# Two mixers: the convolved keys and queries activated and squared at item 28 of the attention loop instead of after it, the filler products dropped, and the result stored in five parts

## The reference, cut to what matters

```
def gated_deltanet(pc, conv_w, a_log, dt_bias, o_norm):
    q, k, v, z, b_in, a_in = split_cols(pc, GDN_SPLITS)
    qkv = silu(causal_dwconv(concatenate([q, k, v]), conv_w))
    q, k, v = split(qkv, 3)
    q = l2_normalize(heads(q), 1e-6) * GDN_HEAD ** -0.5
    k = l2_normalize(heads(k), 1e-6)
    beta = sigmoid(b_in)
    g = -exp(a_log) * softplus(a_in + dt_bias)
    o = chunk_gated_delta_rule(q, k, heads(v), g, beta)
    return rms_norm(o, o_norm) * silu(heads(z))

def l2_normalize(x, eps):
    return x * rsqrt(sum(x * x, axis=-1) + eps)

for l in range(2):
    x = x + 0.5 * swiglu(rms_norm(x) ...)
    x = x + concatenate([attention, rwkv7, gated_deltanet]) @ w_out[l]
    x = x + 0.5 * swiglu(rms_norm(x) ...)
# then two layers of the second block, each of which updates x twice;
# the last one ends with   x = x + g2 * swiglu_2(...)   and x is the output
```

## Time and profile before

| | |
|---|---|
| median of 3 runs | 3575.18 us (3574.53 to 3580.99) |
| profiled execution | 3576.05 us |
| its span, first to last instruction | 3574.3 us |
| PE busy | 3423.1 us (96%) |
| DVE, ACT, POOL busy | 1408.8, 1249.7, 1660.1 us |
| mean granted PE clock | 0.978 of full |
| mixer stretches without tiles | from 575.75 (237.4 us) and from 1766.37 (241.5 us) |
| the store of the result | issued at 3566.68, lands 7.1 us later |

### The profile page before, as it was taken

The page is one execution under the profiler, slowest core; times in us unless marked ns, Lnnn a source line. Parts: engine busy times, 40 slices in busy tenths (PEclk is TensorE's granted clock), DMA queues, the critical chain, the costliest instruction groups (busy, mean ns, idle before and its releaser), DMA issues.

```text
span 3574.3 us, 47700 instructions
## 1 busy us (share of the span) xinstructions
PE 3423.1 (96%) x17140; PEld 2813.0 (79%) x17140; DVE 1408.8 (39%) x2740; ACT 1249.7 (35%) x1881; POOL 1660.1 (46%) x2052
## 2 busy tenths in 40 slices
PE   7999998799999999999878999999899999999999
PEld 6888775688888888887658888888767888888887
DVE  4431477855321322236787442215563110341100
ACT  3222335534222422233463432223533332433321
POOL 5765542004665566644300266644403555435553
PEclk9999998899999999999889999999999999999999
DMA  4443221003443344322100144432202322213222
GB/s 176 145 141 112 83 77 50 16 1 107 148 145 118 118 147 143 125 91 77 65 25 1 57 145 146 135 101 89 77 1 71 100 94 98 73 65 101 99 94 94
DMA packets 100319, 335.25 MB, mean 94 GB/s; under 512 B 10800, under 2 KB 16592, under 8 KB 100064
## 3 DMA queue, kind: packets, MB, share of 16 engines
q1 hardware_dynamic: 83920, 277.83, 23.4%
q10 hardware_dynamic: 16272, 55.65, 4.6%
HBM read 330.78 MB, written 2.65 MB: 93 GB/s over the span
## 4 chain that ended last, share of the span: by engine, by line
issue 40%; POOL 32%; PE 27%; DVE 1%; POOLq 0%; ACT 0%; DVEq 0%
POOL w_lo L654 32%; PE ps L2159 7%; PE ps L2160 7%; PE ps L2161 7%; PE ps L2937 1%; PE ps L2916 0%; PE ps L2182 0%; PE ps L2925 0%; PE ps L2183 0%; PE ps L2187 0%; PE ps L3027 0%; DVE stat L2064 0%; DVE sq L2057 0%; PE ps L3033 0%; PE ps L2917 0%
## 5 line engine op out<-in xcount | busy, mean ns | idle before, releaser
L654 POOL TENSOR_TENSOR w_lo<-w_raw,w_hi 128x256 fp32r<-128x256 f32 x2040 | 1653.4, 843 | 1890.9 <-ACT w_hi L697 1884.3
L2159 PE MATMUL ps<-h_hi,w_hi 128*128 128x512 f32 x2624 | 1030.8, 393 | 0.9 <-ACT mem L899 0.9
L2161 PE MATMUL ps<-h_hi,w_lo 128*128 128x512 f32 x2624 | 1021.6, 389 | 0.0
L2160 PE MATMUL ps<-h_lo,w_hi 128*128 128x512 f32 x2624 | 1021.1, 389 | 0.0
L697 ACT ACTIVATE w_hi<-w_raw 128x1024 fp32r<-128x1024 f32 x510 | 538.5, 1058 | 931.5 <-DMA w_raw<-in_tiles 931.5
L2159 PEld LDWEIGHTS ps<-h_hi,w_hi 128*128 128x128 f32 x2624 | 492.6, 188 | 118.2 <-issue 14.3
L2160 PEld LDWEIGHTS ps<-h_lo,w_hi 128*128 128x128 f32 x2624 | 492.7, 188 | 104.4 <-issue 3.4
L2161 PEld LDWEIGHTS ps<-h_hi,w_lo 128*128 128x128 f32 x2624 | 492.5, 188 | 102.3
L2160 PE MATMUL ps<-a_lo,w_hi 128*128 (+1 forms) x1120 | 435.7, 389 | 0.0
L2159 PE MATMUL ps<-a_hi,w_hi 128*128 (+1 forms) x1056 | 410.8, 389 | 0.0
L2161 PE MATMUL ps<-a_hi,w_lo 128*128 (+1 forms) x1056 | 410.8, 389 | 0.0
(11 more groups left out here) (473 smaller groups left out, 3646.2 us busy)
## 6 DMA issues: line engine op xcount, KB each, us to landing
w_raw<-in_tiles SPq DMA_DIRECT2D x510, 512.0 KB, 3.3
ada_raw<-in_ada_tiles ACTq DMA_DIRECT2D x96, 512.0 KB, 3.3
x<-in_x_t SPq DMA_DIRECT2D x2, 1024.0 KB, 6.4
sq<-in_cond ACTq DMA_DIRECT2D x4, 512.0 KB, 4.0
mem<-gates SPq DMA_DIRECT2D x8, 256.0 KB, 4.0
out_t<-x SPq DMA_DIRECT2D x1, 2048.0 KB, 7.1
consts<-in_consts SPq DMA_DIRECT2D x1, 1280.0 KB, 12.6
core_mem<-gates SPq DMA_DIRECT2D x8, 128.0 KB, 2.8
```

The source lines that it names most:

```text
L654: ins = nc.gpsimd.tensor_tensor(w_lo[:, s, part], w_raw[:, s, part], w_hi[:, s, part].bitcast(F32), ALU.subtract)
L2159: nc.tensor.matmul(bank, wh, hi, start=first, stop=False, skip_group_check=True)
L2160: nc.tensor.matmul(bank, wh, lo, start=False, stop=False, skip_group_check=True)
L2161: return nc.tensor.matmul(bank, wl, hi, start=False, stop=last, skip_group_check=True)
```

## The change

Four things are done, in both layers (the last one once):

- Keys after the convolution go to units 24 and 25 (`U_KG`), free once the convolution is done, and `k * delta` goes to units 9 and 10 (`U_KD`).
- ACT activates and squares keys and queries in `meanwhile(28)` instead of `meanwhile(31)`; the Sqrt table and both roots stay in `meanwhile(31)`.
- PE sums the squares in `meanwhile(29)`, into bank 1, and the 15 filler products are gone. The spread of the keys in `meanwhile(33)` waits for the first inverse ahead of chunk 0 and for the second ahead of chunk 1.
- The result is stored as one DMA of 1 MB (`x` 4 to 7, after the first four updates) and four of 256 KB, each after its own update.

```
-                    if i == 31:
+                    if i == 28:
                         act.wait_ge(S["conv_ready"], l + 1)
                         for at, unit in ((2, U_KG), (0, U_QG)):
                             link(nc.scalar.activation(mem[:, unit:unit + 2, :], core_mem[...], ACT.Silu))
                             nc.scalar.activation(mem[:, U_NORMED + at:...], mem[:, unit:unit + 2, :], ACT.Square).then_inc(S["head_sq"], 1)
+                    if i == 31:
                         load_sqrt()
-                        head_roots(2, 2, 1.0, EPS_NORM, 2)
+                        head_roots(1, 2, 1.0, EPS_NORM, 2)
+                        head_roots(1, 2, 1.0, EPS_NORM)
...
             def recurrences(l, updates):
-                head_roots(3, 2, 1.0, EPS_NORM)
...
+                    if i == 29:
+                        pe.wait_ge(S["g_taken"], l + 1)
+                        for at in (2, 0):
+                            pe.wait_ge(S["head_sq"], due("head_sq"))
+                            head_sums(mem_units(U_NORMED + at, U_NORMED + at + 1), 1, at).then_inc(S["head_sum"], 1)
                     if i == 33:
-                        pe.wait_ge(S["max_ready"], i0 + len(ITEMS))
-                        pe.wait_ge(S["g_taken"], l + 1)
-                        for _ in range(10):
-                            nc.tensor.matmul(ps[:, 1, 0:P], const("ident"), const("ones"), start=True, stop=True)
-                        for at, bank in ((2, 2), (0, 3)):
-                            pe.wait_ge(S["head_sq"], due("head_sq"))
-                            head_sums(...)
-                        for _ in range(5):
-                            nc.tensor.matmul(...)
-                        pe.wait_ge(S["head_inv"], due("head_inv"))
                         for c in range(2):
+                            pe.wait_ge(S["head_inv"], due("head_inv"))
                             head_spread(mem[:, U_NORMED + 2 + c, :], c).then_inc(S["head_spread"], 1)
...
+            sp.wait_ge(S["x_ready"], updated - KD // 2)
+            sp.dma_start(out_t[:, low:high, :], x[:, low:high, :]).then_inc(S["out_stored"], 16)
+            for d, k in enumerate(last_half):
+                sp.wait_ge(S["x_ready"], updated - KD // 2 + d + 1)
+                sp.dma_start(out_t[:, k, :], x[:, k, :]).then_inc(S["out_stored"], 16)
```

More of the change, by code:

```diff
@@ L219, in build_program @@
         soft = mem[ROW_A:ROW_A + 4, 19, :]
-        U_QG, U_KG, U_BONUS, U_DELTA, U_NORMED = 33, 9, 35, 0, 2
+        U_QG, U_KG, U_KD, U_BONUS, U_DELTA, U_NORMED = 33, 24, 9, 35, 0, 2
         def turn_bank(n):
@@ L639, in _ @@
             load_tiles(sines + 1, stream_tiles, SKIPPED["dft_time"])
-            sp.wait_ge(S["x_ready"], KD * sum(n.startswith("ffn") or n.endswith("_out") or "mix_out" in n for n in run))
-            sp.dma_start(out.rearrange("(k p) t -> p k t", p=P), x[:, :, :]).then_inc(S["out_stored"], 16)
+            updated = KD * sum(n.startswith("ffn") or n.endswith("_out") or "mix_out" in n for n in run)
+            out_t = out.rearrange("(k p) t -> p k t", p=P)
+            first_half, last_half = FFN_ORDER[0:KD // 2], FFN_ORDER[KD // 2:]
+            low, high = min(first_half), max(first_half) + 1
+            sp.wait_ge(S["x_ready"], updated - KD // 2)
[3 more added lines that the diff above has]
+                sp.dma_start(out_t[:, k, :], x[:, k, :]).then_inc(S["out_stored"], 16)
             sp.wait_ge(S["vf_moved"], 16)
-            sp.wait_ge(S["out_stored"], 16)
+            sp.wait_ge(S["out_stored"], 16 * (1 + KD // 2))
         @block.gpsimd
@@ L1740, in recurrences @@
                 V.tensor_copy(block_columns(ST_EGL), by_block(eg)[:, :, :, P - 1])
-                V.tensor_tensor(mem[:, 24:26, :], k, mem[:, U_DELTA:U_DELTA + 2, :], ALU.mult).then_inc(S["kd_ready"], 1)
+                V.tensor_tensor(mem[:, U_KD:U_KD + 2, :], k, mem[:, U_DELTA:U_DELTA + 2, :], ALU.mult).then_inc(S["kd_ready"], 1)
                 dve.wait_ge(S["dt_ready"], l + 1)
@@ L1863, in core_step @@
                     V.tensor_tensor(mem[:, 37:39, :], mem[:, U_QG:U_QG + 2, :], mem[:, 41:43, :], ALU.mult)
-                    V.scalar_tensor_tensor(mem[:, 24:26, :], mem[:, 39:41, :], -1.0, mem[:, 41:43, :], ALU.mult, ALU.mult).then_inc(S["gdn_ready"], 1)
+                    V.scalar_tensor_tensor(mem[:, U_KD:U_KD + 2, :], mem[:, 39:41, :], -1.0, mem[:, 41:43, :], ALU.mult, ALU.mult).then_inc(S["gdn_ready"], 1)
                 if n:
@@ L2448, in meanwhile @@
                         ins.then_inc(S["g_turned"], 1)
-                    if i == 33:
-                        pe.wait_ge(S["max_ready"], i0 + len(ITEMS))
-                        pe.wait_ge(S["g_taken"], l + 1)
-                        for _ in range(10):
-                            nc.tensor.matmul(ps[:, 1, 0:P], const("ident"), const("ones"), start=True, stop=True)
-                        for at, bank in ((2, 2), (0, 3)):
-                            pe.wait_ge(S["head_sq"], due("head_sq"))
-                            head_sums(mem_units(U_NORMED + at, U_NORMED + at + 1), bank, at).then_inc(S["head_sum"], 1)
-                        for _ in range(5):
-                            nc.tensor.matmul(ps[:, 1, 0:P], const("ident"), const("ones"), start=True, stop=True)
-                        pe.wait_ge(S["head_inv"], due("head_inv"))
+                    if i == 29:
[3 more added lines that the diff above has]
+                            head_sums(mem_units(U_NORMED + at, U_NORMED + at + 1), 1, at).then_inc(S["head_sum"], 1)
+                    if i == 33:
                         for c in range(2):
+                            pe.wait_ge(S["head_inv"], due("head_inv"))
                             head_spread(mem[:, U_NORMED + 2 + c, :], c).then_inc(S["head_spread"], 1)
@@ L2551, in recurrences @@
                 for at, src in enumerate((*(rw[:, c, 1:] for c in (4, 5, 2, 3)), mem[:, 7, :], mem[:, 8, :],
-                                          mem[:, 37, :], mem[:, 38, :], mem[:, 24, :], mem[:, 25, :])):
+                                          mem[:, 37, :], mem[:, 38, :], mem[:, U_KD, :], mem[:, U_KD + 1, :])):
                     n = due("turn")
@@ L2592, in core_step @@
                 kg, qg = (lambda c: mem[:, U_KG + c, :]), (lambda c: mem[:, U_QG + c, :])
-                qe, kbe = (lambda c: mem[:, 37 + c, :]), (lambda c: mem[:, 24 + c, :])
+                qe, kbe = (lambda c: mem[:, 37 + c, :]), (lambda c: mem[:, U_KD + c, :])
                 nb_t, kt_t, v_t, vb_t, kd_t = (0, 1), (4, 5), (2, 3), (26, 19), (45, 6)
```

## The result

The changed kernel takes 3590.11 us (median of 7 runs, 3588.88 to 3593.06) against 3575.55 us before (7 runs, 3574.53 to 3580.99). The ratio is 1.0036, with a 95% interval of [1.0026, 1.0046]: slower by 14.6 us by the medians and by 9 to 16 by the interval. That is the side that was forecast (3585.3); it is 0.4 us inside the stated range (3578 to 3590.5) and outside the narrower one of the forecast itself (3581 to 3589). The profiled execution has a span of 3588.3 us, 14.0 more than before.

What follows compares the result with a forecast made beforehand. PE is busy 96% of the span, but the change acts where PE waits, at the attention loops' ends and the last store. 7.4 us later in each of two layers minus 4.7 at the store gave 3585.3 us (median), range 3578 to 3590.5.

Steps and rivals of the forecast that it cites:

- The block within the loop: ACT, ahead of item 29: activations, squares and a second table load make item 29 6.8 us late, item 31 at least 5.7.
- the rival with the drain: ACT's table switches in the loop: a drain beside each load costs 2.76 us more a layer, 3590.8 us in all; 2%.
- The sums within the loop: PE, 32 passes ahead of the scores of items 30 and 31: sums end at 650.0, item 31 ends 10.4 us later.
- the third rival: Everything at PE's lower clock, item 31 12.1 us late, last stores in each other's way: +15.4 us, 3590.6; 12%.
- Behind the new E: DVE after E, the end of item 31's exponential: masking delays the inverse; keys' multiplication at E + 8.0, before E + 11.35.
- The decay products: PE, behind the keys' multiplication: 16 passes may still run at the lower clock, 0.3 us a layer added (0 to 0.7).
- The store: End of the kernel: the last 256 KB land in 2.4 us instead of 7.1 for 2 MB, a gain of 4.7 us.
- Sum: Whole kernel: 2 x 7.4 - 4.7 = +10.1 us, 3586.1 for the profiled execution and 3585.3 for the median.
- The first (a clock that stays up): PE's sums in the loop at the upper clock end at 648.3: +2.6 us, 3577.8, no change; 14%.
- The second (a loop that swallows the block): ACT between items 28 and 31 absorbs the block: with no shift of item 31, -11.4 us, 3563.8; 4%.

Runs made afterwards that it cites:

- sums_late: The changed kernel with PE's sums of squares moved back from item 29 to item 33, no fillers, ACT's block staying at item 28; 3580.63 us.
- masks_early: The changed kernel with DVE's 16 masking steps moved from behind item 31 to item 29; 3583.28 us.
- sums_warm: The changed kernel with 10 filler products on PE ahead of the sums at item 29; 3586.46 us.
- masks_warm: The changed kernel with DVE's 16 masking steps moved to item 29 and 10 filler products on PE ahead of the sums there; 3577.62 us.
- store_only: The kernel before with nothing changed but the store in five parts; 3571.71 us.
- warm_core_after: The changed kernel with 38 filler products in each layer on PE ahead of the first core step of the recurrences; 3587.43 us.
- warm_core_best: The kernel before with the store in five parts, no fillers between sums and spread, and 38 fillers ahead of the first core step; 3569.93 us.
- one_filler_block: The kernel before with the store in five parts and without the 5 filler products between sums and spread; 3570.10 us.

## Why the prediction was right, point by point

- **The block within the loop.** Right. Item 29 was to be 6.8 us late and item 31 at least 5.7, because ACT had 1.08 us of idle time to give. In sums_late, where the block is there alone, item 31 was 6.8 late: the idle time took up nothing, since it was a wait for turns on PE, and there PE itself waits for ACT's item 29 and the copy behind it (6.97 us). Each of the two table loads had 0.02 us of gap in front and 0.01 behind, so the rival with the drain falls.
- **The sums within the loop.** Right in kind, too small in size. The step says "I take 650.0, a clock that falls within the first sums", 5.8 us for 32 passes. They took 6.96, since the clock was at 0.50 before the first of them in both layers. I had also let the pieces behind them run partly at the upper clock (3.7 us to item 30); 651.42 to 655.06 is 3.64. So item 31 moved by 11.5 us from item 28 on, where I had 10.4. This is the term that was mis-sized: 1.1 us a layer. (In the prediction's bound for this piece, 2.4 us with 1.87 of it doubled make 4.3 and not 4.1; nothing else hangs on it but the third rival, by 0.2 us a layer.) In layer 0 the clock had been at 0.50 since 638.1, before ACT's block began. In the kernel before it stood at 0.50 from 637.8 too, but rose at 641.2 while PE ran scores; here PE stood idle. In layer 1 it fell at 1846.4, while PE stood idle and waited for the squares.
- **Behind the new E.** Right: E + 8.0 forecast, E + 8.03 measured, with the masking as the last wait before the inverse; masks_early shows it by taking it away. That the number fits to 0.03 us is luck, for two small errors cancel. The first inverse was ready at E + 5.8 and not 6.1. And from the spread's start to the multiplication it took 2.19 us where 1.86 were taken for "the whole spread at the lower level": in the earlier trace rows the clock rose in the middle of the spread, as these stretches of PE before, layer 1, show (the spread ran from 1848.09 to 1850.74; its 16 passes took 2.65 us there and 3.66 in the changed kernel's layer 0, 3.4 of them at 0.50):

```profile
1846.20:1849.50 3.30, 3.30 (x17) 0.50 0.01 2
1849.60:1852.00 2.40, 2.17 (x22) 1.00 0.00 0
```

- **The decay products.** 0.3 us were added; the multiplication of the second chunk came 0.2 later than the first one's shift, and the products ran at 1.00, not at the lower level. Too small to judge.
- **The store.** 2.4 us were forecast for the last part, 2.0 measured; 5.1 us won in place of 4.7. The formula of the Trainium skill (DMA: Bandwidth & Descriptors, Anatomy of one DMA), which is for the GpSimd path, gives 2.6, an estimate; the runs here, which store from SyncE, show 2.0.
- **Sum.** Of the forecast's 14.8 us for the mixers 0.6 were the decay products, which stand behind the multiplication. So 14.2 - 4.7 = +9.5 compares with 16.4 - 5.1 = +11.3 by the table of stretches. That leaves 2.7 us of the 14.0 in stretches for which the prediction had nothing but that 0.6. The time came out inside the stated range only because its upper end was taken from the third rival, which had its excess elsewhere: in a larger shift of item 31 and a smaller gain at the store. With nothing but what the terms measured the forecast would have been 3586.5.
- **The rivals.** Nearest came the third, everything at the lower clock, in the mixers (12.1 us for item 31, 11.5 measured); its clash of the stores did not happen. The first (a clock that stays up) is what the fillers brought about in layer 1 of sums_warm and masks_warm. The second (a loop that swallows the block) was off by the whole block.

**What stays open.** The rest of 2 to 4 us. The stretch from the keys' multiplication to the inverse behind the recurrences took 152.1 and 152.5 us before, 154.1 and 154.2 after. That looks like a cost of the change, but in store_only, whose mixers are those of before, it took 154.3 and 154.1, and in warm_core_after 153.6 and 151.4. But the profiled execution of store_only took 3576.36 us against a median of 3571.71, at a mean granted clock of 0.976; the eight of its twelve executions with 0.977 to 0.980 took 3569.5 to 3572.2 us, the four with 0.975 or 0.976 took 3575.7 to 3578.5. So a few us come and go with the clock in one and the same kernel. The clock in the recurrences is the likely place. In the changed kernel the first core step ran at 0.50 from 690 to 717. Over the 24 recurrences of the twelve profiles, nine were at the lower clock for 42 to 45 us (counted to the first tile behind them) and took 153.9 to 155.4 us up to the inverse; the other fifteen were at it for 20 to 35 us and took 151.4 to 154.3, eleven of them under 153.6. Seven of the nine are in kernels that have ACT's block in the loop. That is a correlation: one profile of each kernel can't tell a lower clock that this change brings about from one that comes and goes; and in warm_core_best 11 us less at the lower clock in each layer than in one_filler_block came with only the 0.5 and 0.8 us above.

## What to carry to other kernels

Work that is moved into a loop of dependent steps can be paid in full however idle the engines look: here the block's 6.8 us were, since the only idle time of its engine was a wait for a step that itself hung on the block. What it uncovered or hid behind the loop has to be read from the waits on the other engines, here 4.3 us of masking that nobody had waited for before. Put such work where the engine that gets it waits for something that does not depend on the work. Take fillers out one group at a time: of the two groups that this change dropped, the second cost 1.2 and 0.8 us and the first saved 3 us of sums. And split the last store: with 2.0 us for 256 KB against 7.1 for 2 MB it won 5 us by itself.

## What the runs showed of the hardware that was not expected

Head sums (128 x 2 outputs, two passes each) keep PE busy by the record but did not raise the clock: 32 of them in a row ran at 0.50 for 6.9 us in both layers of the changed kernel, with PE busy 6.87 of 6.90 us. The same passes took 0.12 to 0.13 us at 1.00 (3.98 us for 32 in one_filler_block, behind fillers) and 0.22 us at 0.50. This is not peculiar to products with two columns, for in the recurrences of the changed kernel, with products of 64 and 128 columns, the clock stayed down as well:

```profile
690.00:717.00 27.00, 26.84 (x144) 0.51 0.00 1
```

So a record of PE that is busy throughout does not tell that the clock is up; the granted clock has to be read beside it. And 38 fillers did not protect what came after them: the clock fell from 1.00 to 0.50 between 688 and 698 in warm_core_after, with PE busy 8.05 of these 10 us, the first 2 of which it waited.
